# A hybrid streaming encoder step on one core: the windowed attention is cut by pairs of heads and interleaved with the query projection

## The chip, the cores and the metric

The kernel runs on one core of one Trainium2 chip. The metric is the device time of one execution in microseconds (us). An execution is one launch; TensorE (PE), VectorE (DVE), ScalarE (ACT), GpSimd (POOL) and the DMA queue of SyncE (SP) each follow their own instruction list and meet only at semaphores.

## The reference, cut to what matters

One step of a two-layer encoder over 256 prompt frames and 64 new frames (T = 320 tokens, 1024 channels). Layer 0 is a recurrent mixer and a mixture of experts (MoE); layer 1 is attention over a window of three chunks of 64 frames, with 16 query heads on 4 key/value heads and a learned sink per head, and again a MoE.

```python
def sink_probs(s, sink, mask):
    m = jnp.maximum(jnp.max(s, axis=-1, keepdims=True), sink)
    e = jnp.exp(s - m)
    return e / (jnp.sum(e, axis=-1, keepdims=True) + jnp.exp(sink - m))

def window_attn(h, pos, k, v, past_k, past_v, p, j):
    q = (h @ p['at_w_q'][j] + p['at_b_q'][j]).reshape(B, S, N_HEADS, HEAD_DIM)
    q = rope_partial(q, pos)
    ...            # scores of each 64-frame chunk with its own and the two chunks before it
    probs = sink_probs(s, sink, mask)
    o = jnp.einsum('bnkgqs,bnskd->bnqkgd', probs, vb)
    return o.reshape(B, T, H * hd) @ p['at_w_o'][j] + p['at_b_o'][j]
```

The 320 tokens are five chunks (n = 0 to 4): the prompt's four, which see 64, 128, 192 and 192 keys, and the new frames' one, which sees 192 (128 cached, 64 own).

## The kernel before, in words

Everything is stored with channels on the 128 partitions: the residual is `x[:, c, :]` with C = 8 blocks of 128 channels and 320 tokens. A block of queries holds two heads of 64, a pair. Each engine's work is one hand-written list in one function; a helper notes under which key an instruction counts its engine's semaphore up, and `wait(key)` waits for that count. So the order of the code is the order on each engine, and an engine that waits holds up all that stands behind it. `bank.open` hands out the eight PSUM banks in turn.

In the profile every matmul of TensorE has the line L677 (the helper `mm`), transposes have their own (L1180 for the probabilities), every ACT operation L1224, and DVE's L1477 (tensor with tensor), L1480 (tensor with scalar) and L1483. A 32-bit matmul shows as two records. The form "128*128 128x320" is a 128 by 128 weight tile and an operand of 320 columns; "64*64" and "128*64" are smaller tiles of the array.

Layer 1's mixer goes like this:

- The keys are rotated, turned and copied (until about 869 us).
- `project("q", [c], ...)` makes the queries of pair c: 8 matmuls, 16 records. ACT adds the bias (`qraw`), `q_turn(c)` multiplies by the constant matrix `ropep` on TensorE, and DVE finishes the rotation with three operations (`q ready`). TensorE runs the eight projections first, each turn one pair behind.
- Then the five chunks. `scores(n)` makes the scores of chunk n for all 16 heads. DVE `row_maxima(n)` takes maxima and adds the sink, ACT `exps(n)` takes 8 exponentials and one of the sink, DVE divides, TensorE turns the probabilities 64 keys at a time (`attended(n)`, first half), ACT copies the turned blocks `pT` out of PSUM, TensorE multiplies by the values `v64` (second half), ACT copies the result to `oT`. TensorE's list holds `scores(n + 1)` ahead of `attended(n)`.
- `project("ao", ...)`, the output projection, waits for all of `oT`; then the MoE of layer 1.

The DMA queue of SP loads the second half of the output projection's weights and the first experts' weights when the query weights have been used.

## Time and profile before

| what | value |
|---|---|
| time before, median of 3 runs | 1338.46 us (1337.78 to 1346.84) |
| profiled execution | 1344.89 us, of which the span of its instructions 1343.1 us |
| TensorE busy in the span | 1150.3 us (86%), mean granted clock 0.93 |
| DVE, ACT busy | 540.1 us (40%), 343.9 us (26%) |
| query projection to output projection | 869.5 to 973.6 us |

The span runs from the first to the last instruction of the profiled execution; the rest of its time lies around it. Busy shares are means over stages with different limits, so a change in one stage has to be read in that stage. The granted clock is TensorE's: 1.00 is 2.4 GHz, 0.50 is 1.2 GHz, and a number between is a stretch that holds both.

### The profile page before, as it was taken

To read this page: it belongs to the slowest core of one execution; us is meant where nothing else is said; L and a number is where in the kernel's file an instruction comes from. 1 tells how busy PE (TensorE), PEld (TensorE's weight loads), DVE (VectorE), ACT (ScalarE), POOL (GpSimd) and SP (SyncE) were. 2 spreads that over 40 slices of the span, in tenths; PEclk is the share of its full clock that TensorE was granted. 3 is DMA by queue.
4 is the path that set the end of the run, shared out by engine and by line. 5 is a ranking of instruction groups with operands and counts; after the bars stand their busy time and mean duration, and the time that the engine had idled before them with its cause. 6 is when DMAs were issued, how large, how long until landed. Compare 5 with 4: busy or idle time off the path is not lost.

```text
span 1343.1 us, 23574 instructions
## 1 busy us (share of the span) xinstructions
PE 1150.3 (86%) x9621; PEld 675.5 (50%) x9621; DVE 540.1 (40%) x1412; ACT 343.9 (26%) x652; POOL 57.0 (4%) x67
## 2 busy tenths in 40 slices
PE   5579998888988878689999997897795899999995
PEld 2146665565767744434444443575672534444433
DVE  3422193333331254524444544325227235444444
ACT  1122230121111201223333223215303232323322
POOL 2000000000000000001000001000000000000100
PEclk9789998999898988889999999898697999999997
DMA  9533115867674144039999997006022079999941
GB/s 250 164 125 126 63 62 197 292 232 263 227 256 182 39 189 180 1 125 418 429 423 426 425 380 259 6 6 251 1 94 94 0 320 423 427 426 422 424 184 39
DMA packets 45992, 297.19 MB, mean 221 GB/s; under 512 B 5972, under 2 KB 7352, under 8 KB 22360
## 3 DMA queue, kind: packets, MB, share of 16 engines
q1 hardware_dynamic: 43856, 290.17, 54.4%
q0 software_dynamic: 1856, 5.79, 1.9%
q8 instruction: 63, 1.03, 0.3%
q10 hardware_dynamic: 200, 0.06, 0.0%
q14 instruction: 17, 0.14, 0.0%
HBM read 293.77 MB, written 2.24 MB: 220 GB/s over the span
## 4 chain that ended last, share of the span: by engine, by line
PE 75%; DMA 10%; DVE 9%; ACT 3%; issue 2%; SPq 0%; ACTq 0%; DVEq 0%; POOL 0%; POOLq 0%
PE bank L677 73%; DMA ring<-in_ada_w 8%; DVE work L1477 3%; ACT work L1224 2%; DMA ring<-in_kv_ada_w 1%; DVE work L1483 1%; DVE work L1480 1%; DVE rstd L1515 1%; DVE x_res L1850 1%; DMA ring<-in_rw_w_rkv 1%; PE bank L1055 1%; DVE work L1836 1%; DVE ring L1477 1%; DVE att L1927 1%; DVE work L1589 0%
## 5 line engine op out<-in xcount | busy, mean ns | idle before, releaser
L677 PE MATMUL bank<-ring,work 128*64 128x512 f32 (+1 forms) x1760 | 354.5, 558 | 9.3 <-DVE work L1836 7.6
L677 PE MATMUL bank<-work,ring 128*128 128x320 f32 (+3 forms) x1600 | 300.3, 366 | 31.6 <-DVE work L1477 8.9
L677 PE MATMUL bank<-work 128*128 128x320 bf16 (+7 forms) x1842 | 238.7, 304 | 49.0 <-DVE work L1757 13.9
L677 PEld LDWEIGHTS bank<-work,ring 128*128 128x128 f32 (+2 forms) x1600 | 214.0, 173 | 118.5 <-issue 29.3
L677 PEld LDWEIGHTS bank<-work 128*128 128x128 bf16 (+2 forms) x1842 | 178.3, 132 | 118.0 <-issue 34.3
L677 PEld LDWEIGHTS bank<-ring,work 128*64 128x64 f32 (+1 forms) x1760 | 120.7, 141 | 220.7 <-issue 213.7
L1224 ACT ACTIVATE work<-bank 128x320 f32<-128x320 f32 (+6 forms) x116 | 59.1, 550 | 259.8 <-PE bank L677 234.2
L677 PE MATMUL bank<-ring 64*64 64x64 f32 (+2 forms) x2624 | 104.7, 234 | 2.0 <-issue 2.0
L677 PEld LDWEIGHTS bank<-ring 64*64 64x64 f32 (+2 forms) x2624 | 94.9, 145 | 22.8 <-issue 19.0
L677 PE MATMUL bank<-ring,cs 128*32 128x512 f32 x448 | 66.8, 675 | 34.9 <-DMA ring<-in_ada_w 29.0
L1850 DVE SCALAR_TENSOR_TENSOR x_res<-bank,mod,x_res 128x256 f32<-128x256 f32 (+1 forms) x256 | 86.2, 378 | 18.4 <-PE bank L677 4.6
L1830 DVE SCALAR_TENSOR_TENSOR work<-work,small,bank 128x256 f32<-128x256 f32 x32 | 21.5, 672 | 174.2 <-ACT work L1388 88.9
L1224 ACT ACTIVATE ring<-bank 128x512 f32<-128x512 f32 (+3 forms) x67 | 37.7, 563 | 191.0 <-PE bank L677 189.9
L1843 DVE TENSOR_TENSOR work<-bank,work 128x512 f32<-128x512 f32 x64 | 44.1, 689 | 61.9 <-ACT work L1392 61.9
L1477 DVE TENSOR_TENSOR ring<-ring,bank 128x512 f32<-128x512 f32 x45 | 29.1, 685 | 84.0 <-PE bank L677 84.0
L631 POOL TENSOR_TENSOR work<-work 128x512 bf16<-128x512 f32 x32 | 36.4, 1159 | 547.4 <-ACT work L1396 547.4
L1392 ACT ACTIVATE work<-bank 128x512 bf16<-128x512 f32 x64 | 38.1, 596 | 49.3 <-PE bank L677 49.3
L1483 DVE SCALAR_TENSOR_TENSOR work<-work,vec 128x320 f32<-128x320 f32 x56 | 27.0, 547 | 52.9 <-PE bank L677 52.6
L1376 ACT COPY work<-work 128x512 f32 x64 | 39.3, 623 | 14.1 <-issue 14.1
L677 PEld LDWEIGHTS bank<-ring,cs 128*32 128x32 f32 x448 | 10.9, 112 | 62.6 <-DMA ring<-in_ada_w 42.4
L1396 ACT ACTIVATE work<-work 128x512 bf16<-128x512 f32 x64 | 40.1, 626 | 8.6 <-DVE work L1843 8.6
L1224 ACT ACTIVATE work<-x_res 128x640 f32<-128x640 f32 x20 | 14.7, 736 | 98.0 <-DVE x_res L1483 45.5
(183 smaller groups left out, 757.6 us busy)
## 6 DMA issues: line engine op xcount, KB each, us to landing
ring<-in_moe_w_gu SPq DMA_DIRECT2D x64, 2048.0 KB, 13.3
ring<-in_moe_w_down SPq DMA_DIRECT2D x64, 1024.0 KB, 13.8
ring<-in_ada_w SPq DMA_DIRECT2D x40, 1024.0 KB, 5.3
ring<-in_rw_w_rkv SPq DMA_DIRECT2D x6, 2048.0 KB, 7.7
ring<-in_ada_w SPq DMA_DIRECT2D x4, 2048.0 KB, 28.5
ring<-in_kv_ada_w SPq DMA_DIRECT2D x8, 1024.0 KB, 5.1
ring<-in_rw_w_o SPq DMA_DIRECT2D x2, 2048.0 KB, 11.4
ring<-in_at_w_q SPq DMA_DIRECT2D x2, 2048.0 KB, 13.8
```

What stands on the lines that cost most here:

```text
L631: eng.tensor_tensor(dpart[:, 0, 2, cols], rest[:, n, :], dpart[:, 0, 1, cols], ALU.subtract).then_inc(S["lo_ready0"], 1)
L677: return eng.matmul(out, l, r, start=start, stop=stop, **kw)
L1055: ins = eng.transpose(ps[0][:, 2 * P * u + P * f:2 * P * u + P * f + P], hid[:, u, P * f:P * f + P], ident)
L1224: ac.did(eng.activation(out, in_, f, **kw), *keys)
L1376: eng.copy(xe[:, u, :, 64 * v:64 * v + 64], xall[:, :, bass.ds(at, SLOTS)]).then_inc(S["xe_ready"], 1)
L1392: eng.activation(dpart[:, u, 0, 512 * n:512 * n + 512], ps[4 + n][:, :], ACT.Copy).then_inc(S["hi_ready"], 1)
L1396: eng.activation(dpart[:, u, 1, 512 * n:512 * n + 512], rest[:, n, :], ACT.Copy).then_inc(S["mid_ready"], 1)
L1477: op(eng.tensor_tensor(out, a, b, o_), *keys)
L1483: op(eng.scalar_tensor_tensor(out, a, s_, b, o1, o2), *keys)
L1830: eng.scalar_tensor_tensor(hid_w[:, u], silu[:, u, :].rearrange("p (q f) -> p q f", f=2), wslot[:, u:u + 1], ps[3 + 4 * u][:, FE:2 * FE].r ...
L1843: eng.tensor_tensor(rest[:, n, :], ps[4 + n][:, :], dpart[:, u, 0, 512 * n:512 * n + 512], ALU.subtract).then_inc(S["rest_ready"], 1)
L1850: ins = eng.scalar_tensor_tensor(x[:, c, t0:t0 + n], ps[(6, 1, 2)[c % 3]][:, t0:t0 + n], mod[:, l, r, 40 + c:40 + c + 1], x[:, c, t0:t0 + ...
```

## The change

The attention loop now runs over the eight pairs of heads instead of over the five chunks, and is mixed into the loop of the projections. Step s of the new loop does, on TensorE: the projection of pair s, the turning of the probabilities of pair s - 3 (`prob_turn`), the rotation matmul of pair s - 1, the scores of pair s - 2 for all five chunks, and the product with the values of pair s - 3 (`attended`). ACT and DVE have matching loops. Three steps behind the last projection (s = 8, 9, 10) finish the last three pairs.

With it, data is laid out anew: the values are kept as tiles of 128 tokens (`vtok`) where a chunk's window holds a pair of key chunks, so that a window of 192 keys is one part of 128 (`PAIR`) and one of 64 (`LONE`); a pair's probabilities for all chunks are one row of 768, in two buffers; eight transposes turn them, four of 128 and four of 64 columns, and ACT copies them out in two operations. The negated sink is computed once (`nsink`), so that three small DVE operations per chunk become one per pair, and ACT adds the sink as a bias. `oT` moves to another buffer, and the output projection waits for it block by block. Two of the stores to DRAM become one, so the counts of `out_written` drop by 16.

```diff
+SPAN = [(0, 64, 0, 0), (0, 128, 0, 64), (0, 192, 1, 0), (64, 256, 1, 192), (256, 448, 0, 192)]
+PCOL = [0, 64, 384, 576, 192]
+VTILES = [(0, 128), (64, 128), (128, 128), (192, 64), None, (256, 64)]
+PAIR = [None, (0, 0), (0, 1), (1, 2), (4, 3)]
+LONE = [(0, 0), None, (2, 1), (3, 2), (5, 3)]
...
-        hkv, haq, q, qt, oT = E[1], E[5], E[6], E[7], E[5]
+        hkv, haq, q, qt, oT = E[1], E[5], E[6], E[7], E[1]
...
-        v64 = work[0:64, 4 * B:4 * B + 7 * 256].rearrange("p (n d) -> p n d", n=7)
+        vtok = work[:, 4 * B:4 * B + 6 * 256].rearrange("p (n d) -> p n d", n=6)
...
-        prob2 = [work[:, a:a + 1536].rearrange("p (c s) -> p c s", c=C) for a in (0, 7 * B)]
-        pT = work[0:64, 1536:1536 + 3072].rearrange("p (w c s) -> p w c s", w=3, c=C)
+        prob2 = [work[:, a:a + 768] for a in (0, 768)]
+        qrot2 = [work[:, a:a + T] for a in (1536, 1536 + T)]
+        pT2 = [work[:, 7 * B + a:7 * B + a + 1024].rearrange("p (w n s) -> p w n s", w=2, n=4) for a in (0, 1024)]
...
-            for c in range(C):
-                project("q", [c], haq, lambda hf: ("wq", hf), ("h", "A1"))
-                if c:
-                    q_turn(c - 1)
-            q_turn(C - 1)
-            pe.wait("kswapped", 1)
-
-            def scores(n):
...
+            def scores(c):
+
+                g = c // 2
+                pe.wait("q ready", c)
+                for b in range(2):
+                    pb = bank.open("score", c, b)
+                    for n, (lo, hi, at, col) in enumerate(SPAN):
...
                         for h in range(2):
...
-                            ins = mm(pb[r, 256 * cc:256 * cc + hi - lo], q[r, c, t0:t0 + CH],
+                            ins = mm(pb[r, col:col + hi - lo], q[r, c, CH * n:CH * n + CH],
                                      kT[r, var + g // 2, lo:hi], True, True)
...
-            def attended(n):
...
-            scores(0)
-            for n in range(NCH):
-                if n + 1 < NCH:
-                    scores(n + 1)
-                attended(n)
-            pe.wait("oT", NCH - 1)
-            project("ao", range(C), oT, lambda hf: ("ao", hf))
...
+            def prob_turn(c):
+
+                pe.wait("prob", c)
+                prob = prob2[c % 2]
+                pb = bank.open("pT", c, 0)
+                for n in range(1, NCH):
+                    ins = eng.transpose(pb[:, P * (n - 1):P * n], prob[:, PCOL[n]:PCOL[n] + P], ident)
+                full(ins, "pT", c, 0)
+                pb = bank.open("pT", c, 1)
+                for k, n in enumerate((0, 2, 3, 4)):
+                    a = PCOL[n] + (P if n else 0)
+                    ins = eng.transpose(pb[0:64, P * k:P * k + P], prob[:, a:a + 64], ident)
+                full(ins, "pT", c, 1)
+
+            def attended(c):
+
+                g = c // 2
+                pe.wait("pT ready", c)
+                pT = pT2[c % 2]
+                pb = bank.open("o", c)
+                for k, table, w in ((P, PAIR, 0), (64, LONE, 1)):
+                    for n in range(NCH):
+                        if table[n] is None:
+                            continue
+                        tile, at = table[n]
+                        for h in range(2):
+                            ins = mm(pb[64 * h:64 * h + 64, CH * n:CH * n + CH],
+                                     vtok[0:k, tile, 64 * g:64 * g + 64], pT[0:k, w, at, 64 * h:64 * h + 64],
+                                     w == 0 and n == 1, w == 1 and n == NCH - 1)
+                full(ins, "o", c)
+
+            pe.wait("kswapped", 1)
+            pe.wait("vtok")
+            for s in range(C + 3):
+                if s < C:
+                    project("q", [s], haq, lambda hf: ("wq", hf), ("h", "A1"))
+                if s >= 3:
+                    prob_turn(s - 3)
+                if 1 <= s <= C:
+                    q_turn(s - 1)
+                if 2 <= s <= C:
+                    scores(s - 2)
+                if s >= 3:
+                    attended(s - 3)
+                if s == C:
+                    scores(C - 1)
+            project("ao", range(C), oT, lambda hf: ("ao", hf), ("oT",))
...
-            for c in range(C):
...
-            def exps(n):
...
-            exps(0)
-            for n in range(NCH):
-                parts = min(n + 1, 3) if n < 4 else 3
-                for w in range(3):
-                    if w == 2 and n + 1 < NCH:
-                        exps(n + 1)
...
+            def exps(c):
+
+                prob, att = prob2[c % 2], att2[:, c % 2]
+                ac.wait("row max", c)
+                for n, (lo, hi, b, col) in enumerate(SPAN):
+                    act(prob[:, PCOL[n]:PCOL[n] + hi - lo], ps[seen_bank(("score", c, b))][:, col:col + hi - lo],
+                        ACT.Exp, ("read", "score", c, b), ("exp", c), bias=att[:, 1, n:n + 1], scale=SCALE,
+                        accum_out=att[:, 2, n:n + 1])
+                act(att[:, 3, 0:NCH], att[:, 1, 0:NCH], ACT.Exp, ("sink exp", c), bias=sink[:, c:c + 1])
+
+            for s in range(C + 3):
+                if s < C:
+                    act(q[:, s, :], pk("q", s)[:, 0:T], ACT.Identity, ("read", "q", s), ("qraw", s),
+                        bias=vcol("at_b_q", s))
+                if s >= 3:
+                    c = s - 3
+                    pT = pT2[c % 2]
+                    act(pT[:, 0], pk("pT", c, 0)[:, :].rearrange("p (n s) -> p n s", n=4), ACT.Copy,
+                        ("read", "pT", c, 0))
+                    act(pT[0:64, 1], pk("pT", c, 1)[0:64, :].rearrange("p (n s) -> p n s", n=4), ACT.Copy,
+                        ("read", "pT", c, 1), ("pT ready", c))
+                if s == C:
+                    exps(C - 2)
+                if s >= 3:
+                    act(oT[:, s - 3, :], pk("o", s - 3)[:, 0:T], ACT.Copy, ("read", "o", s - 3), ("oT", s - 3))
+                if 2 <= s < C:
+                    exps(s - 2)
+                if s == C:
+                    exps(C - 1)
...
-            for c in range(C):
-                tt_(qt[:, c, :], acst("sin"), pk("qrot", c)[:, 0:T], M, ("read", "qrot", c))
+            eng.wait_ge(in_sems["sink_in"], 32)
...
+            def rotated(c):
+
+                tt_(qrot2[c % 2], acst("sin"), pk("qrot", c)[:, 0:T], M, ("read", "qrot", c))
                 tt_(q[:, c, :], q[:, c, :], acst("cos"), M)
                 ve.settle()
-                tt_(q[:, c, :], q[:, c, :], qt[:, c, :], A_, ("q ready", c))
-            eng.wait_ge(in_sems["sink_in"], 32)
-
-            def row_maxima(n):
...
-                stt(att[:, 1, :], att[:, 0, :], SCALE, sink[:, :], M, ALU.max)
...
-                ts(att[:, 1, :], att[:, 1, :], -1.0, None, M, ALU.bypass)
...
-                tt_(att[:, 4, :], sink[:, :], att[:, 1, :], A_, *[("row max", n, b) for b in range(4)])
-
-            row_maxima(0)
-            for n in range(NCH):
-                W = min(n + 1, 3) * CH if n < 4 else 192
...
+            def row_maxima(c):
+
+                att = att2[:, c % 2]
+                a, b = [pk("score", c, k) for k in range(2)]
+                for n, w, col in ((0, 64, 0), (1, 128, 64), (4, 192, 192)):
+                    op(eng.tensor_reduce(att[:, 0, n:n + 1], a[:, col:col + w], AX.X, ALU.max))
+                op(eng.tensor_reduce(att[:, 0, 2:4], b[:, 0:384].rearrange("p (n s) -> p n s", n=2), AX.X, ALU.max))
+                ve.settle()
+                ts(att[:, 1, 0:NCH], att[:, 0, 0:NCH], -SCALE, nsink[:, c:c + 1], M, ALU.min, ("row max", c))
...
+            def normalized(c):
+
+                prob, att = prob2[c % 2], att2[:, c % 2]
+                ve.wait("sink exp", c)
+                tt_(att[:, 5, 0:NCH], att[:, 2, 0:NCH], att[:, 3, 0:NCH], A_)
...
+                op(eng.reciprocal(att[:, 5, 0:NCH], att[:, 5, 0:NCH]))
...
+                for n, (lo, hi, _b, _col) in enumerate(SPAN):
+                    a = slice(PCOL[n], PCOL[n] + hi - lo)
+                    ts(prob[:, a], prob[:, a], att[:, 5, n:n + 1], None, M, ALU.bypass, ("prob", c))
+
+            for s in range(1, C):
+                rotated(s - 1)
+                if s >= 2:
+                    row_maxima(s - 2)
+                    normalized(s - 2)
+            rotated(C - 1)
+            for c in (C - 2, C - 1):
+                row_maxima(c)
+            for c in (C - 2, C - 1):
+                normalized(c)
```

TensorE's order before, from the last two projections (`work,ring` 128x320) over the rotation matmuls (`work,const_phase`) to the scores and products of the first chunks (64x64 to 64x192) and the turnings (L1180):

```order
L677 MATMUL bank<-work,ring 128x320 x8
L677 MATMUL bank<-work,const_phase 128x320
L677 MATMUL bank<-work,ring 128x320 x8
L677 MATMUL bank<-work,const_phase 128x320 x2
L677 MATMUL bank<-work 64x64 x16
L677 MATMUL bank<-work 64x128 x16
L1180 MATMUL bank<-const,work 64x128 x8
L677 MATMUL bank<-work 64x128 x8
L677 MATMUL bank<-work 64x192 x16
```

All projections stand ahead of all attention, and the turnings of a chunk ahead of its product. In the changed kernel, step s = 7, the last of the five full ones, from its projection to the next step's first turnings (L1183 and L1188 are the two sizes of turnings):

```order
L686 MATMUL bank<-work,ring 128x320 x8
L1183 MATMUL bank<-const,work 128x128 x4
L1188 MATMUL bank<-const,work 64x128 x4
L686 MATMUL bank<-work,const_phase 128x320
L686 MATMUL bank<-work 64x64 x2
L686 MATMUL bank<-work 64x128 x2
L686 MATMUL bank<-work 64x192 x6
L686 MATMUL bank<-work 64x64 x16
L1183 MATMUL bank<-const,work 128x128 x4
```

Turnings, rotation, scores and products of three different pairs now stand between two projections. What remains behind the last one, from the products of pair 5 with the scores of pair 7 to the output projection (`work,ring` x64):

```order
L686 MATMUL bank<-work 64x64 x18
L686 MATMUL bank<-work 64x128 x2
L686 MATMUL bank<-work 64x192 x6
L1183 MATMUL bank<-const,work 128x128 x4
L1188 MATMUL bank<-const,work 64x128 x4
L686 MATMUL bank<-work 64x64 x16
L1183 MATMUL bank<-const,work 128x128 x4
L1188 MATMUL bank<-const,work 64x128 x4
L686 MATMUL bank<-work 64x64 x16
L686 MATMUL bank<-work,ring 128x320 x64
```

The last two pairs' turnings and products stand there with nothing between them. On ACT before, one chunk's exponentials (`work,att`) and its sink, then copies of turned probabilities (64x512) and of the result (128x8x64):

```order
L1224 ACTIVATE work,att<-bank,att 128x192 x8
L1224 ACTIVATE att<-att 128x8
L1224 ACTIVATE work<-bank 64x512 x2
L1224 ACTIVATE work<-bank 128x8x64
L1224 ACTIVATE work<-bank 64x512 x4
```

Here the exponentials of a chunk stand ahead of most copies of the chunk before. On ACT in the changed kernel, step s = 7: bias of the queries, two copies of turned probabilities, copy of the result (128x320), five exponentials and the sink:

```order
L1245 ACTIVATE work<-bank,vec 128x320
L1245 ACTIVATE work<-bank 128x512
L1245 ACTIVATE work<-bank 64x512
L1245 ACTIVATE work<-bank 128x320
L1245 ACTIVATE work,att<-bank,att 128x64
L1245 ACTIVATE work,att<-bank,att 128x128
L1245 ACTIVATE work,att<-bank,att 128x192 x3
L1245 ACTIVATE att<-att,sink 128x5
```

The copy of one pair's result now stands ahead of the next pair's exponentials.

## Rows read from the trace of the kernel before

**Rows 1.** The page: span, TensorE's busy time and share.

```profile
span 1343.1 us, 23574 instructions
PE 1150.3 (86%) x9621; PEld 675.5 (50%) x9621; DVE 540.1 (40%) x1412; ACT 343.9 (26%) x652; POOL 57.0 (4%) x67
```

**Rows 2.** Windows by stage: length, busy time (instructions) of each engine, PEclk, DMA share, GB/s.

```profile
869.50:908.00 38.50, 38.42 (x144) 26.83 (x143) 8.47 (x19) 4.99 (x12) 3.17 (x6) 1.00 0.05 11
908.00:962.00 54.00, 38.42 (x357) 32.13 (x359) 23.77 (x91) 27.79 (x107) 0.00 (x0) 0.77 0.39 157
962.00:974.00 12.00, 10.54 (x98) 9.11 (x96) 0.00 (x0) 4.52 (x8) 0.00 (x0) 0.76 0.01 1
```

**Rows 3.** Chain that ended last, in order of time: start us, us, what.

```profile
869.55 38.24 PE bank L677 x142
...
937.68 3.33 ACT work L1224 x16
...
942.10 9.67 PE bank L677 x76
951.76 0.03 issue
...
951.89 1.96 DVE att L1927 x4
...
973.56 39.04 PE bank L677 x144
```

**Rows 4.** Windows of single TensorE runs between chunks, columns as in Rows 2.

```profile
924.80:926.90 2.10, 1.99 (x17) 1.67 (x16) 1.83 (x4) 1.39 (x3) 0.00 (x0) 1.00 0.87 367
...
942.10:951.80 9.70, 9.70 (x81) 8.63 (x82) 1.40 (x7) 0.60 (x1) 0.00 (x0) 0.56 0.01 2
951.60:953.70 2.10, 2.00 (x17) 1.67 (x16) 1.81 (x4) 1.37 (x3) 0.00 (x0) 1.00 0.00 0
...
958.90:964.80 5.90, 5.90 (x49) 5.57 (x50) 1.40 (x7) 0.00 (x0) 0.00 (x0) 0.50 0.00 0
...
969.70:972.90 3.20, 3.11 (x48) 2.86 (x48) 0.00 (x0) 0.01 (x1) 0.00 (x0) 1.00 0.03 5
```

**Rows 5.** Timeline, one projection, its rotation and the next: start, us, engine line op.

```profile
878.54 4.47 PE L677 MATMUL bank<-work,ring 128*128 128x320 f32 x16
...
882.85 0.70 PE L677 MATMUL bank<-work,const_phase 128*128 128x320 f32 x2
...
883.39 4.47 PE L677 MATMUL bank<-work,ring 128*128 128x320 f32 x16
883.59 0.49 DVE L1477 TENSOR_TENSOR work<-const_phase,bank 128x320 f32<-128x320 f32 x1 [3.43 <-PE bank L677]
...
884.51 0.49 DVE L1477 TENSOR_TENSOR work<-work 128x320 f32<-128x320 f32 x1
```

**Rows 6.** Timeline, small matmuls at full clock and the weight loads after a change of tile.

```profile
908.59 0.92 PE L677 MATMUL bank<-work 64*64 64x64 f32 x24
...
924.85 1.67 PEld L1180 LDWEIGHTS bank<-const,work 128*64 128x64 f32 x16 [0.28 <-issue]
924.85 1.94 PE L1180 MATMUL bank<-const,work 128*64 128x128 f32 x16
```

**Rows 7.** Groups by form, 869.5 to 973.6 us: busy us, mean ns, idle before.

```profile
L677 PE MATMUL bank<-work 64*64 64x192 f32 x96 | 13.9, 446 | 0.0
...
L1927 DVE TENSOR_REDUCE att<-bank 128x2 f32<-128x384 f32 x12 | 5.9, 550 | 10.8 <-PE bank L677 10.8
L1480 DVE TENSOR_SCALAR work<-work,att 128x192 f32<-128x192 f32 x24 | 5.8, 315 | 0.1
...
L1942 DVE RECIPROCAL att<-att 128x8 f32<-128x8 f32 x5 | 1.0, 203 | 0.2
...
L1224 ACT ACTIVATE work<-bank 64x512 f32<-64x512 f32 x24 | 12.8, 590 | 14.1 <-PE bank L1180 14.0
...
L1224 ACT ACTIVATE work<-bank,vec 128x320 f32<-128x320 f32 x8 | 4.2, 527 | 33.5 <-PE bank L677 33.5
...
L1224 ACT ACTIVATE att<-att 128x8 f32<-128x8 f32 x5 | 1.2, 242 | 0.0
```

**Rows 8.** DMA queue of SP and landing times of the output projection's weights.

```profile
907.27 0.37 SPq L485 DMA_DIRECT2D ring<-in_at_w_o  x1
...
ring<-in_at_w_o SPq DMA_DIRECT2D x2, 2048.0 KB, 14.1
```

More of the change, by code:

```diff
@@ L263, in build @@
         sink = sb("sink", [P, C])
+        nsink = sb("nsink", [P, C])
         att2 = sb("att", [P, 2, 6, C])
@@ L655, in _ @@
                 put(o[n_out][0, t0:t0 + 64].rearrange("t n d -> t (n d)"), k64[:, w, :])
-            pl.wait("v64")
-            for n_out, w, t0 in ((5, 2, 0), (5, 3, 64), (9, 6, 0)):
-                put(o[n_out][0, t0:t0 + 64].rearrange("t n d -> t (n d)"), v64[:, w, :])
+            pl.wait("vtok")
+            put(o[5][0].rearrange("t n d -> t (n d)"), vtok[:, 2, :])
+            put(o[9][0].rearrange("t n d -> t (n d)"), vtok[0:64, 5, :])
             cleared(1)
@@ L1132, in _ @@
             pe.wait("vT", 1)
-            for w, t0 in enumerate((0, 64, 128, 192, 256)):
-                pb = bank.open("v64", w)
+            for w, tile in enumerate(VTILES):
+                if tile is None:
+                    continue
+                t0, k = tile
+                pb = bank.open("vtok", w)
                 for c in range(2):
-                    ins = eng.transpose(pb[0:64, P * c:P * c + P], vT[:, c, t0:t0 + 64], ident)
-                full(ins, "v64", w)
+                    ins = eng.transpose(pb[0:k, P * c:P * c + P], vT[:, c, t0:t0 + k], ident)
+                full(ins, "vtok", w)
             for w, t0 in enumerate((128, 192, 384)):
@@ L1424, in _ @@
                 act(kT[:, 2 + c, :], pk("kswap", c)[:, 0:448], ACT.Copy, ("read", "kswap", c), ("kswapped", c))
-            for w in range(5):
-                act(v64[:, w if w < 4 else 6, :], pk("v64", w)[0:64, 0:256], ACT.Copy, ("read", "v64", w), ("v64",))
+            for w, tile in enumerate(VTILES):
+                if tile is not None:
+                    act(vtok[0:tile[1], w, :], pk("vtok", w)[0:tile[1], 0:256], ACT.Copy, ("read", "vtok", w),
+                        ("vtok",))
             for w in range(3):
@@ L1428, in _ @@
                 act(k64[:, w, :], pk("k64", w)[0:64, 0:256], ACT.Copy, ("read", "k64", w), ("k64",))
-            for c in range(C):
-                act(q[:, c, :], pk("q", c)[:, 0:T], ACT.Identity, ("read", "q", c), ("qraw", c),
-                    bias=vcol("at_b_q", c))
-            def exps(n):
-                W = min(n + 1, 3) * CH if n < 4 else 192
-                prob, att = prob2[n % 2], att2[:, n % 2]
-                for b in range(4):
-                    ac.wait("row max", n, b)
-                    for cc in range(2):
-                        c = 2 * b + cc
-                        act(prob[:, c, 0:W], ps[seen_bank(("score", n, b))][:, 256 * cc:256 * cc + W], ACT.Exp,
-                            ("read", "score", n, b), ("exp", n, c), bias=att[:, 1, c:c + 1], scale=SCALE,
-                            accum_out=att[:, 2, c:c + 1])
-                act(att[:, 3, :], att[:, 4, :], ACT.Exp, ("sink exp", n))
```

64 lines of the change are left out of this document (9 added, 55 removed).

## The prediction

> **What bounds the kernel now.** I read the page first [rows 1]: TensorE is busy for 86% of the span, but that is a mean over many stages. The windows by stage come next [rows 2]. In the query projection TensorE is busy for 38.42 of 38.50 us at full clock; nothing can be gained there without taking work away. In the 66 us behind it TensorE is busy for 49 us, at a granted clock of 0.77 and 0.76, while DVE (23.8 us) and ACT (27.8 + 4.5 us) are idle for more than half. The chain of waits [rows 3] says why: it runs from TensorE to DVE's maxima to ACT's exponentials and back, chunk by chunk, and no engine has another chunk's work to fill with. From the first projection (869.55) to the output projection (973.56) it is 104.0 us. The third thing is the clock [rows 4]: from 942.1 to 951.8 TensorE is busy throughout but mostly at half clock, and from 958.9 to 964.8 wholly at half clock, both right behind a pause. A clock of 0.77 over 54 us and 0.76 over 12 us means that about 46% of the 66 us ran at 1.2 GHz.
>
> **The change: work of a full step at full clock.** From one projection to the next is 4.85 us for 18 equal records [rows 5], so 16 records of projection are 4.3 us and a rotation 0.54 us. Turnings: 16 took 1.94 us [rows 6], so 8 are 0.95 us; there are 64 in place of 96. The scores keep their columns: 768 keys for 2 heads in 2 records each. At full clock 48 records of 128 columns took 3.11 us [rows 4], 0.032 us for 64 columns (0.038 by the 24 records in 0.92 us of [rows 6], which contain the last one's own length). 48 such units are 1.55 us. The products with the values fall from 256 records of 128 columns to 256 of 64 over the whole stage; 32 a step make 1.05 us, if the two heads of a pair run side by side as they do in those rows.
>
> New is that the size of the array's tile changes within a step: into the scores, into the products of 128 keys, into those of 64, and back to the projection. The nearest row is the weight loader's pause of 0.28 us between 64*64 and 128*64 tiles [rows 6]. Part of such a pause is the usual spacing, so I take 0.1 us each, between 0 and 0.28. The step is 4.3 + 0.95 + 0.54 + 1.55 + 1.05 + 0.4 = 8.8 us.
>
> The Trainium skill, page "TensorEngine Tiling", section "Tiling Modes" (Key Properties), says that a change of tiling mode, unlike one of the tile alone, makes TensorE drain. The pause of 0.28 us is in line with a short drain. If each drain showed the whole length of a small record, 0.446 us [rows 7], the four would cost 1.8 us a step in place of 0.4, and the gain below would be about 8 us smaller.
>
> **The chain of a full step.** TensorE may finish its own work early and still wait for the next probabilities, so I follow one pair from the start of its neighbour's rotation matmul (0). DVE begins 0.74 us later (882.85 to 883.59) and needs 1.41 us for three operations (883.59 to 884.51 + 0.49) [rows 5]: 2.15. The scores end on TensorE at 0.54 + 0.1 + 1.55 = 2.2. The reductions, one of 0.55 us [rows 7] and three smaller, overlap a little: I put 1.15, and 0.2 for the sink: 3.5. The products end at 3.45, and ACT's list has the copy of their result, 0.53 us [rows 7], ahead of the exponentials: ACT is free at 4.1. Eight exponentials of 192 keys take 3.33 us [rows 3], 0.42 each; three of these and two smaller are 1.9, and the sink's 0.24 [rows 7] brings 6.25. DVE adds, takes the reciprocal (0.2) and divides five times, 0.24 each (24 in 5.8 us) [rows 7]: 7.8. The turnings follow, 0.95: 8.75. Chain and TensorE's own work are level, so the step is 8.8 us, and each of the two hides the other. If only the chain grew, by a longer product for instance, it would show in full. The copies of turned probabilities, 2 x 0.59 us [rows 7], lie beside rotation and scores (2.1 us).
>
> **The whole stage.** Fill: three projections and a rotation put the second pair's rotation at 13.45; the first chain lacks the copy ahead of the exponentials and ends at 20.65, TensorE's fourth projection at 19.95; with the turnings the third rotation stands at 21.6. Four steps of 8.8 lead to 56.8, where the last full step's rotation stands; pair 5's probabilities are ready at 64.6. TensorE has had nothing since 60.25, a pause of 4.35 us.
>
> Behind the projections: turnings 0.95, rotation 0.54, scores of pair 6 1.65, products of pair 5 1.15, scores of pair 7 1.55, that is 70.4; maxima 1.45 with the delay, exponentials 2.15: 74.0. ACT copies pair 6's turned probabilities only then (1.2), products 1.15, turnings of pair 7 0.95, their copies 0.9 past the end, products 1.15: 79.4. The output projection can start, since it needs pair 7 only for its eighth matmul. At full clock the gain is 104.0 - 79.4 = 24.6 us.
>
> Then the clock. That tail holds 9.1 us of TensorE work in 15 us, behind a pause of 4.35 us. Before, with pauses like that, 46% of the stage ran at half clock [rows 2]; I take two thirds for the tail, +6.1 us, and 1.5 us for the start of the output projection, of which a first block of 4.3 us would be 8.6. The ends are 0 and 9.1 + 4.3. Gain: 24.6 - 7.6 = 17 us.
>
> **What moves and costs nothing.** The second half of the output weights is loaded when the last query weights have been used, at 907.27 before [rows 8], some 55.6 us into the stage now, about 925. They land 14.1 us later, and the fifth block of the output projection comes 17 us behind its start at 957: covered by 35 us. The experts' first loads stand behind it on SP's queue and move by the same 18 us, with over 100 us to their use. GpSimd's two stores in place of three leave at a time when nothing waits for them. TensorE's new wait for the copied values ahead of the projections has the projections behind it; the copies ran beside the turnings before, so I put 0, at most the 0.4 us of one copy. Waiting for `oT` block by block costs nothing. A PSUM bank comes round after eight openings, and a step has seven, so each was read a step earlier.
>
> **The sum.** The profiled execution took 1344.89 us with a span of 1343.1, 6.4 us above the median of 1338.46; the gain belongs to one stage, and I take it off both. Profile: span 1343.1 - 17 = 1326; median 1321.5.
>
> **Rivals.**
> *The clock holds in the tail.* Before, it was still at 1.00 in a short run of turnings right behind scores (951.6 to 953.7) [rows 4]. Then the gain is 24.6 us: 1314. Against it stands the long pause.
> *The step is longer.* If the two heads' products don't overlap where 128 rows of the array are used (+1.05 us), or tile changes cost 0.28 and more (+0.7), a step is 9.5 to 10.5 us, since products and tile changes lie on the chain as well; over six steps the gain falls by 4 to 10 us: 1326 to 1332. That is what the page on tiling would make of it.
> *Half clock in the full steps* (the slower side). The projections no longer stand together; between them are 4.5 us of small tiles, and small tiles ran at 0.50 and 0.56 in [rows 4]. At half clock a step's TensorE work would be 17 us, 8.4 more. Two of the five steps eat the gain; all five give 1321.5 + 42 = 1363. Against it: those rows began behind a pause, half of each step is full-size projection, which ran at 1.00 [rows 2], and turnings behind scores held 1.00 twice [rows 4].
> *It doesn't interleave*: some wait puts one pair's chain behind the other's, so that a step takes 8.8 plus the chain's other half, 4 us; five steps more or less return the gain: 1338.
>
> **How the numbers follow.** Forecast 0.48, the clock holds 0.22, longer steps 0.18, half clock in the steps 0.06, no interleaving 0.06. The likeliest is 1321.5. The bounds are a gain of 27 us (no tile costs, full clock) and of about 1 us (every bound at its bad end at once); 8 in 10 reach from 1313 to 1333. About 1%, 13.4 us, is what a measurement of this kernel can tell from no change. Faster by over that: 0.22 + 0.44 of the forecast's 0.48 + 0.03 of the longer steps' = 0.69; within it 0.04 + 0.15 + 0.06 = 0.25; slower 0.06.
>
> **What would show it.** Right: the stage from the first query projection to the output projection is 85 to 90 us; full steps repeat every 8.8 us with TensorE's clock at 1.00; a pause of some 4 us stands behind the last projection, and the clock is at half in the tail. Maxima, exponentials and divisions of each pair lie under the next projection. Wrong: steps above 9.5 us, with TensorE waiting for DVE's divisions ahead of the turnings; half clock during projections; or a change outside the stage, which I have put at nothing.

## The result and the profile after

| kernel, in one comparison | median | runs | range |
|---|---|---|---|
| before | 1338.36 us | 4 | 1337.78 to 1346.84 |
| changed | 1324.91 us | 4 | 1324.00 to 1325.82 |

The ratio is 0.987, with an interval of 0.9846 to 0.9894: faster, by 13.5 us by these medians, where 17 were forecast. The profiled execution took 1324.0 us, and its page begins so:

```profile
span 1321.8 us, 23637 instructions
...
PE 1131.9 (86%) x9653; PEld 659.4 (50%) x9653; DVE 542.0 (41%) x1424; ACT 341.3 (26%) x650; POOL 56.4 (4%) x66
```

TensorE's share of the span is 86% as before [rows 1]; its busy time fell by 18.4 us and the span by 21.3. The page doesn't tell where, so the stage comes next. From the first record of the query projection to the first of the output projection it was 869.39 to 973.56, 104.2 us; now it is 868.83 to 952.38, 83.6 us. The windows by stage (length, busy us and instructions of PE, PEld, DVE, ACT and POOL, then TensorE's granted clock, DMA share, GB/s):

```profile
869.00:890.80 21.80, 20.93 (x96) 14.55 (x96) 5.64 (x18) 6.31 (x20) 2.73 (x5) 1.00 0.08 19
890.80:925.30 34.50, 34.50 (x315) 25.45 (x314) 17.03 (x60) 16.03 (x61) 0.00 (x0) 1.00 0.00 1
925.30:932.70 7.40, 3.31 (x55) 2.29 (x54) 4.23 (x15) 3.23 (x14) 0.00 (x0) 1.00 0.98 361
932.70:943.00 10.30, 7.24 (x82) 5.35 (x82) 5.54 (x21) 5.08 (x22) 0.00 (x0) 0.83 1.01 427
943.00:952.30 9.30, 7.87 (x80) 6.32 (x80) 1.51 (x8) 3.55 (x10) 0.00 (x0) 0.52 0.36 147
952.30:957.00 4.70, 4.70 (x13) 3.05 (x10) 0.00 (x0) 0.44 (x1) 0.00 (x0) 0.50 0.00 0
957.00:993.70 36.70, 36.66 (x137) 25.55 (x135) 10.78 (x28) 4.23 (x5) 0.00 (x0) 1.00 0.31 119
```

The first line is the fill, the second the full steps: 34.5 us in which TensorE never stops, at full clock, with 17 us of DVE and 16 of ACT beside it. Before, 54 us of attention held 38 us of TensorE work at 0.77 [rows 2]. Then come three lines of tail, with pauses in the first two and half clock in most of the last two, and one in which the output projection still starts at 0.50.

The timeline of TensorE (start, us, instructions, idle time before and who ended it) shows a step and the tail:

```profile
889.88 0.66 PE L1183 MATMUL bank<-const,work 128*128 128x128 f32 x4 [0.87 <-DVE work L1504]
...
898.54 0.60 PE L1183 MATMUL bank<-const,work 128*128 128x128 f32 x4
898.97 0.60 PE L1188 MATMUL bank<-const,work 128*64 128x128 f32 x4
899.41 0.70 PE L686 MATMUL bank<-work,const_phase 128*128 128x320 f32 x2
900.04 2.75 PE L686 MATMUL bank<-work 64*64 64x64 f32 x52
902.73 4.57 PE L686 MATMUL bank<-work,ring 128*128 128x320 f32 x16
907.14 0.60 PE L1183 MATMUL bank<-const,work 128*128 128x128 f32 x4
...
932.78 0.86 PE L1183 MATMUL bank<-const,work 128*128 128x128 f32 x4 [4.17 <-DVE work L1504]
...
943.07 0.91 PE L1183 MATMUL bank<-const,work 128*128 128x128 f32 x4 [3.06 <-DVE work L1504]
...
945.52 2.17 PE L686 MATMUL bank<-work 128*64 128x64 f32 x32 [0.68 <-ACT work L1245]
...
952.38 32.94 PE L686 MATMUL bank<-work,ring 128*128 128x320 f32 x113
```

From turnings to turnings a step is 8.60 us (898.54 to 907.14). No record in it has an idle time. Only the first turnings (0.87 us, the fill) and those behind the last projection (4.17 and 3.06 us) wait for DVE's divisions at L1504. The same group of 32 products takes 2.17 us here that takes 1.30 us at full clock (below). The output projection starts without waiting for anything. How close the other side of a step is shows on DVE:

```profile
905.79 1.14 DVE L1504 TENSOR_SCALAR work<-work,att 128x64 f32<-128x64 f32 x5
...
914.39 1.14 DVE L1504 TENSOR_SCALAR work<-work,att 128x64 f32<-128x64 f32 x5
```

The divisions end at 906.93 and the turnings begin at 907.14; the next pair's end at 915.53 and its turnings begin at 915.74. That is 0.21 us, of which some 0.05 also lie between the two where the turnings do wait (914.28 to 914.32 in the longer chain below). So the chain of a pair is done 0.1 to 0.2 us before TensorE comes to it.

### The profile page after: what moved, and what is told of

Same layout as the page of the kernel before. It is cut to its first block, busy times and chain, and to the rows that moved or that the text cites. A ratio compares the mean times of both kernels' runs of the same rounds, so it can differ in the third digit from the quotient of the medians.

```text
span 1321.8 us, 23637 instructions
## 1 busy us (share of the span) xinstructions
PE 1131.9 (86%) x9653; PEld 659.4 (50%) x9653; DVE 542.0 (41%) x1424; ACT 341.3 (26%) x650; POOL 56.4 (4%) x66
## 3 DMA queue, kind: packets, MB, share of 16 engines
q8 instruction: 64, 1.05, 0.3%
## 4 chain that ended last, share of the span: by engine, by line
PE 75%; DMA 11%; DVE 9%; ACT 2%; issue 2%; SPq 0%; ACTq 0%; DVEq 0%; POOL 0%; POOLq 0%
PE bank L686 73%; DMA ring<-in_ada_w 9%; DVE work L1501 2%; DMA ring<-in_kv_ada_w 2%; ACT work L1245 1%; DVE work L1507 1%; DVE work L1504 1%; DVE rstd L1539 1%; DVE x_res L1874 1%; DMA ring<-in_rw_w_rkv 1%; PE bank L1064 1%; DVE work L1860 1%; DVE ring L1501 1%; DVE work L1613 0%; PE bank L1231 0%
## 5 line engine op out<-in xcount | busy, mean ns | idle before, releaser
L686 PE MATMUL bank<-work 128*128 128x320 bf16 (+7 forms) x1906 | 227.0, 284 | 41.8 <-DVE work L1781 13.9
L686 PEld LDWEIGHTS bank<-work 128*128 128x128 bf16 (+3 forms) x1906 | 166.8, 126 | 113.2 <-issue 39.7
L1245 ACT ACTIVATE work<-bank 128x320 f32<-128x320 f32 (+6 forms) x111 | 55.8, 537 | 252.4 <-PE bank L686 235.8
## 6 DMA issues: line engine op xcount, KB each, us to landing
ring<-in_moe_w_gu SPq DMA_DIRECT2D x64, 2048.0 KB, 13.5
```

Of the source, the lines that this page charges most:

```text
L686: return eng.matmul(out, l, r, start=start, stop=stop, **kw)
L1245: ac.did(eng.activation(out, in_, f, **kw), *keys)
```

## The experiments

The table reads each run's trace at the same three points: the first record of the query projection, the first of the output projection, and the last. "At half" is the length times twice what the granted clock lacks to 1.00, that is, the time at 1.2 GHz. The ratio is to the kernel before, run beside it.

| kernel | first projection at | stage, us | at half, us | output projection, us | median us | ratio, interval |
|---|---|---|---|---|---|---|
| before | 869.39 | 104.2 | 30.7 | 34.7 | 1338.36 | 1 |
| changed | 868.83 | 83.6 | 12.5 | 37.0 | 1324.91 | 0.987 (0.9846 to 0.9894) |
| before, again | 867.81 | 104.2 | 30.7 | 34.7 | 1343.33 | one run |
| pairs apart | 870.20 | 91.0 | 16.5 | 36.7 | 1327.30 | 0.985 (0.9812 to 0.9886) |
| warm tail | 872.54 | 78.7 | 0 | 34.7 | 1320.19 | 0.981 (0.978 to 0.9834) |
| longer chain | 873.50 | 90.5 | 16.0 | 36.9 | 1333.36 | 0.990 (0.9863 to 0.9933) |
| changed, again | 863.64 | 83.6 | 12.5 | 37.0 | 1323.22 | 0.986 (0.982 to 0.9899) |
| early output | 863.86 | 78.7 | 0 | 28.3 | 1308.82 | 0.976 (0.9723 to 0.9805) |
| before, warm | 867.07 | 95.0 | 0 | 34.7 | 1333.62 | 0.993 (0.9904 to 0.9957) |
| more tile changes | 871.07 | 90.1 | 12.2 | 37.1 | 1327.50 | 0.989 (0.986 to 0.9922) |
| pairs apart, warm | 867.89 | 88.9 | 3.4 | 34.7 | 1325.97 | 0.988 (0.9845 to 0.9921) |

The stage repeats within 0.1 us in the two profiles of the kernel before and in the two of the changed kernel. Where it begins does not: 868.83 and 863.64 us in the two executions of the changed kernel, up to 873.50 in the others. The kernel before had medians of 1338.36, 1346.81, 1342.93 and 1340.51 us in the four comparisons. So sizes below are told by the stage, and by the median only where it can tell.

One difference lies outside stage and output projection. These are the windows from 39.0 us (before) and 41.3 us (changed) behind the start of the output projection, which is the same place in both programs, to the end:

```profile
1012.60:1343.10 330.50, 283.49 (x1468) 133.18 (x1468) 148.80 (x454) 101.13 (x173) 20.84 (x20) 0.94 0.66 277
...
993.68:1321.80 328.12, 281.25 (x1468) 132.52 (x1468) 148.93 (x454) 101.12 (x173) 20.82 (x20) 0.95 0.67 279
```

This part, mostly the MoE, is 2.4 us shorter with the same 1468 records of TensorE and a granted clock of 0.95 instead of 0.94. It repeats: from the end of the output projection to the end of the span it is 334.8 us in both profiles of the kernel before and 332.5 in both of the changed one, 2.3 us less. No run shows why the clock is higher there.

### The kernel before and the changed kernel, each once more

No edit.

> The unchanged kernel before, for a second profile. The profiled executions of before and after differ by 20.9 us (1344.89 and 1324.0), the medians by 13.5. Theory A: the execution of before that was profiled lost its 6.5 us over the median in the attention stage, by half clock; then this one, if its time is near 1338, shows the stage from the first query projection to the output projection at 97 to 99 us in place of 104.0, with less than 30 us at half clock. Theory B: the 6.5 us lie in other stages; then the stage is again 103 to 105 us while the span is near 1336.5, and the gain in the stage (20.6 us) is partly given back by half clock at the start of the output projection (about 2 us) and the rest is chance in the clock elsewhere.

The kernel before in windows of the stage and of the output projection, columns as above:

```profile
867.81:971.97 104.16, 87.08 (x594) 67.78 (x592) 32.22 (x109) 37.37 (x126) 3.16 (x6) 0.85 0.22 85
971.97:1006.70 34.73, 34.73 (x129) 24.59 (x130) 9.02 (x21) 2.21 (x3) 0.00 (x0) 1.00 0.23 91
```

The stage came back with the same length and the same clock. This execution took 1343.3 us, though, and not the 1338 that theory A asked for, so it can't rule A out by itself. It is 1.6 us shorter than the first, and its stage begins 1.6 us earlier. The clearer case is the changed kernel: its two profiled executions differ by 5.1 us (1324.0 and 1318.9), its stage begins 5.2 us earlier in the second, and is equally long. So what varied between the profiled executions of one kernel lies ahead of the stage, as theory B had it.

> The changed kernel unchanged, timed in more rounds beside the kernel before. In the first comparison the medians differ by 13.5 us; in the last job the kernel before ran between 1338 and 1349, median 1346.8, while its stage was 104.2 us in both profiles. Theory: the stage gains 20.6 us less 2.3 for the output projection's start at half clock in every execution, and the executions of either kernel vary by some 10 us ahead of the stage, so with more runs the difference of the medians is 16 to 22 us. Rival: the gain depends on the execution (half clock in the stage by chance), then stage lengths differ between profiles of the same kernel by more than 2 us and the difference stays at 13 to 14.

The changed kernel's stage was 83.6 us again, and the output projection 37.0. Its median, 1323.22 (1318.70 to 1326.55), is 19.7 us under that of the kernel before in the same comparison, 1342.93 (1336.07 to 1351.63), where the first comparison gave 13.5. From the first projection to the end of the output projection the gain is 138.9 - 120.5 = 18.4 us; with the 2.3 us behind it, 20.7 us from the first projection to the end of the span, above both medians' differences. The two comparisons' medians thus differ by 6 us, the two pairs of profiles, from the first projection on, by 0.1.

### Pairs, but not interleaved

All projections and rotations first, then pair after pair, the scores of one ahead of the turnings of the one before; ACT's and DVE's lists follow that order:

```diff
+            for c in range(C):
+                project("q", [c], haq, lambda hf: ("wq", hf), ("h", "A1"))
+                if c:
+                    q_turn(c - 1)
+            q_turn(C - 1)
+            scores(0)
+            for c in range(C):
+                if c + 1 < C:
+                    scores(c + 1)
+                prob_turn(c)
+                attended(c)
```

> All eight projections first, as in the kernel before, then the pairs, each pair's scores ahead of the turnings of the pair before; all else as in the changed kernel. Theory: the gain comes from the projections as cover. A pair's cycle without cover is divisions 1.55, maxima 1.45 and exponentials 2.15, 5.2 us, in which TensorE has 3.6 us of work at full clock and 7.2 at half; eight pairs of 5.5 to 7 us, 5 us ahead and 4 behind, on top of 38.4 us of projections: stage 92 to 103 us, time 1327 to 1338, TensorE at half clock for most of the pairs. Rival: cutting by pairs alone (fewer turnings, fewer columns in the products) makes the gain: then the time is at or below 1325.

TensorE's timeline of the first pairs and of two later ones:

```profile
916.60 0.66 PE L1183 MATMUL bank<-const,work 128*128 128x128 f32 x4 [4.28 <-DVE work L1496]
...
918.56 4.72 PE L686 MATMUL bank<-work 128*64 128x64 f32 x52 [0.68 <-ACT work L1243]
...
936.85 2.60 PE L686 MATMUL bank<-work 128*64 128x64 f32 x52 [0.73 <-ACT work L1243]
940.48 0.66 PE L1183 MATMUL bank<-const,work 128*128 128x128 f32 x4 [1.03 <-DVE work L1496]
...
945.92 0.66 PE L1183 MATMUL bank<-const,work 128*128 128x128 f32 x4 [1.02 <-DVE work L1496]
```

The stage is 91.0 us, just under the 92 to 103 that my theory allowed, and 16.5 us of it ran at half clock, not most of the pairs. A pair takes 5.44 us (940.48 to 945.92), of which TensorE waits 1.03 for the divisions and 0.73 for ACT's copies. The pairs with their new layout, not interleaved, bring 13.2 of the 20.6 us of the stage; mixing them into the projections brings the other 7.4. This run doesn't part the smaller unit from the layout that came with it.

### The clock held in the tail

Matmuls whose results nobody reads fill the two pauses, seven ahead of pair 5's turnings and five ahead of pair 6's:

```diff
+            def warm(k, n):
+                pb = bank.open("warm", k)
+                for _ in range(n):
+                    ins = mm(pb[:, 0:T], acst("ropep"), q[:, 0, :], True, True)
...
+                if s in (C, C + 1):
+                    warm(s - C, (7, 5)[s - C])
```

> The changed kernel with matmuls whose result nobody reads in the two pauses behind the last projection: 7 (14 records of 128x320) ahead of pair 5's turnings and 5 ahead of pair 6's. Theory: the pauses of 4.2 and 3.1 us bring TensorE to half clock for 17 us; filled, the clock stays at 1.00, the tail from 928.5 to the output projection shrinks from 23.9 to some 19 us, and the projection's start is no longer at half clock: 5 to 7 us less, 1318 to 1320. Rival: the small tiles and turnings of the tail bring it down whatever stands in the pauses, or the fillers delay the turnings: 1324 to 1327.

The filling and the turnings behind it on TensorE, then a product of the tail:

```profile
932.22 4.04 PE L686 MATMUL bank<-work,const_phase 128*128 128x320 f32 x14
936.46 0.65 PE L1183 MATMUL bank<-const,work 128*128 128x128 f32 x4 [0.21 <-DVE work L1514]
...
946.96 1.30 PE L686 MATMUL bank<-work 128*64 128x64 f32 x32 [0.72 <-ACT work L1255]
```

With 24 more records on TensorE the stage is 4.9 us shorter and the output projection 2.3 us: the product takes 1.30 us instead of 2.17. Pair 5's turnings begin 6.93 us behind the start of the scores ahead of them, as in the changed kernel (929.53 to 936.46, 925.85 to 932.78), and still wait 0.21 us: its divisions came no earlier and the filling held nothing up. What was won is the clock behind the pauses.

### A chain one microsecond longer

Three more exponentials of 192 keys, into a spare buffer, ahead of each pair's own:

```diff
+                for n in (2, 3, 4):
+                    lo, hi, b, col = SPAN[n]
+                    act(work[:, a3 + ...], ps[seen_bank(("score", c, b))][:, col:col + 192], ACT.Exp, ("spare", c, n),
+                        bias=att[:, 1, n:n + 1], scale=SCALE)
```

> The changed kernel with three more exponentials of 192 keys per pair on ACT, ahead of the needed ones, into a spare buffer: about 1.0 us more on the chain of each pair, nothing more on TensorE. Theory: chain and TensorE's own work are level within 0.2 us in a full step, so a step grows from 8.6 to 9.4 us and a pause of 0.8 us stands ahead of each turnings; with the first chain and two in the tail 6 to 8 us more: 1331 to 1333. Rival: the chain has slack to spare (TensorE alone bounds the step): only first chain and tail grow, 2 to 3 us, 1327 to 1328.

Two starts of TensorE's turnings with the rotation behind the first, and the divisions ahead of the second in the chain of waits:

```profile
904.90 0.66 PE L1183 MATMUL bank<-const,work 128*128 128x128 f32 x4 [0.60 <-DVE work L1509]
...
905.83 0.70 PE L686 MATMUL bank<-work,const_phase 128*128 128x320 f32 x2
...
914.32 0.66 PE L1183 MATMUL bank<-const,work 128*128 128x128 f32 x4 [0.60 <-DVE work L1509]
```

```profile
913.13 1.15 DVE work L1509 x5
914.28 0.04 issue
914.32 0.66 PE bank L1183 x4
```

The step is 9.42 us instead of 8.60, and now the divisions are waited for in each. From the rotation to the divisions it is 7.30 us (905.83 to 913.13) where it was 6.38 (899.41 to 905.79). So of 0.92 us put on the chain 0.1 went into its slack and 0.8 showed in the step. The stage grew by 6.9 us, within the 6 to 8 expected for chain and TensorE being level; the median of 1333.4 is just above the 1331 to 1333.

### Six more tile changes a step

The same products, in an order in which 128 keys and 64 keys alternate:

```diff
-                for k, table, w in ((P, PAIR, 0), (64, LONE, 1)):
-                    for n in range(NCH):
+                for n in (1, 0, 2, 3, 4):
+                    for k, table, w in ((P, PAIR, 0), (64, LONE, 1)):
```

> The changed kernel with the products of 128 and of 64 keys in turn, chunk by chunk, in place of all of 128 and then all of 64: 6 more changes of the array's tile per pair, 48 in all, and the same records. Theory: a change costs 0.1 us (records start 0.25 us apart where 0.16 is usual), so a pair's products grow by 0.5 to 0.7 us, a full step from 8.6 to 9.2, the stage from 83.6 to 88: 1329 to 1331. Rival, a full drain at each change: 0.28 us and more each, a step of 10.2 or more, 1337 to 1340. Third: changes are free, 1325.

Scores and products of a step on TensorE, and the turnings of two steps:

```profile
911.14 0.60 PE L1183 MATMUL bank<-const,work 128*128 128x128 f32 x4
...
912.64 3.63 PE L686 MATMUL bank<-work 64*64 64x64 f32 x52
...
920.62 0.60 PE L1183 MATMUL bank<-const,work 128*128 128x128 f32 x4
```

The 52 records take 3.63 us instead of 2.75, and the step 9.48 instead of 8.60. Six changes cost 0.88 us, 0.147 each, against 0.1 taken in the prediction and the 0.28 of its upper bound. Nothing was added but the order. The 0.88 us are more than the 0.5 to 0.7 expected, so step and stage (9.48 and 90.1 us) are longer than the 9.2 and 88 expected, while the median, 1327.5, lies under the 1329 to 1331 (a difference that the starts of the stage can make). By the Trainium skill, page "TensorEngine Tiling (Array Packing)", section "Tiling Modes" (Key Properties), a change of tiling mode drains TensorE; the trace agrees that a change costs, at about a third of a record's 0.446 us [rows 7].

### The clock held in the kernel before, and in pairs apart

Idle matmuls as above: in the kernel before six ahead of the first chunk's turnings and one to three ahead of each chunk's product; in pairs apart seven ahead of the first pair's turnings, then one ahead of each pair's turnings and one ahead of its products.

```diff
+            def warm(pb, k):
+                for _ in range(k):
+                    mm(pb[:, 0:T], acst("ropep"), q[:, 0, :], True, True)
...
+                        pb = bank.open("pT", n, w, hf)
+                        if n == 0 and hf == 0:
+                            warm(pb, 6)
...
+                pb = bank.open("o", n)
+                warm(pb, (1, 3, 3, 3, 1)[n])
                 pe.wait("pT ready", n)
-                pb = bank.open("o", n)
```

> The kernel before with idle matmuls in most of its pauses of TensorE, written into the PSUM bank that the waiting work will overwrite: 6 ahead of the first chunk's turnings, 1 to 3 ahead of each chunk's product. Theory: of its 104.2 us stage, 30.7 at half clock, TensorE's runs at half clock cost 10 to 13 us, and with the clock held the stage is 91 to 95 us, as short as the pairs without cover (91.0); so much of what cutting by pairs gains is the clock. Rival: the products of 64 keys on half of the array's rows keep the clock at half whatever stands ahead of them, or the chain of engines sets the length: 100 to 105 us.

> The pairs behind the projections (no interleaving), with idle matmuls in TensorE's pauses: 7 ahead of the first pair's turnings, then one ahead of each pair's turnings and one ahead of its products. With the clock held in all three, the stages would be 95.0 us (kernel before with idle matmuls), X here, 78.7 us (changed kernel with idle matmuls). Theory: cutting by pairs shortens the cycle by itself, from fewer turnings, narrower products, fewer small operations on DVE and equal pairs; without cover a pair's cycle is 5.45 us and X is 87 to 89: about 7 us from the pairs, 9 from the projections as cover. Rival: without the half clock the pairs bring nothing over the chunks, X is 93 to 96, and their 13 us in the stage were the clock alone.

Two products of the kernel before behind their filling, on TensorE:

```profile
925.41 1.88 PE L677 MATMUL bank<-work,const_phase 128*128 128x320 f32 x6 [1.92 <-ACT work L1231]
927.23 4.56 PE L677 MATMUL bank<-work 64*64 64x128 f32 x64
...
937.10 1.88 PE L677 MATMUL bank<-work,const_phase 128*128 128x320 f32 x6 [0.18 <-ACT work L1231]
938.94 5.43 PE L677 MATMUL bank<-work 64*64 64x128 f32 x80
```

And the chain of waits of two pairs in pairs apart, warm:

```profile
919.73 0.67 PE bank L1188 x4
...
920.43 2.90 ACT work L1249 x12
...
924.35 0.78 DVE work L1502 x3
...
925.18 0.67 PE bank L1188 x4
...
925.87 2.90 ACT work L1249 x12
```

The run of TensorE that took 9.7 us in the kernel before [rows 4] takes 5.4, and the stage 95.0 instead of 104.2. One filling cost time of its own: that of chunk 1 could start only when its PSUM bank was free (925.41, behind a pause of 1.92), when ACT's copies for the products had ended 1.2 us before, and put the products off by 1.82 us to 927.23. Without it the stage would be up to 1.8 us shorter, an estimate from these two rows. In pairs apart the stage went from 91.0 to 88.9, within the 87 to 89 expected: its pairs still repeat every 5.44 us (920.43 to 925.87), set by ACT's copy and exponentials, the divisions and the first turnings, one behind the other, which no filling shortens. With the clock held, or nearly (3.4 us at half are left in pairs apart), the three ways stand at 93.2 to 95.0 (chunks), 88.9 (pairs) and 78.7 us (pairs among projections).

### Work of the next stage in the pauses

The last run puts useful work where the idle matmuls were: twelve matmuls of the output projection, on the pairs that are done by then, in two PSUM banks that are kept until pairs 6 and 7 are added.

```diff
+                if s == C:
+                    early(0, range(0, 5))
+                    early(1, range(0, 2))
+                if s == C + 1:
+                    early(1, range(2, 5))
+                    early(0, [5])
+                    early(1, [5])
...
+            for m in range(2):
...
+                for c in (6, 7):
+                    pe.wait("oT", c)
+                    ins = mm(ps[seen_bank(("ao", m))][:, 0:T], ..., oT[:, c, :], False, c == 7)
...
+            project("ao", range(2, C), oT, lambda hf: ("ao", hf), ("oT",))
```

> The changed kernel with part of the output projection moved into the two pauses behind the last query projection: 7 matmuls of its first two blocks ahead of pair 5's turnings, 5 ahead of pair 6's; the two PSUM banks are held until the blocks are finished. Theory: the pauses are filled with useful work, the clock stays at 1.00 as with the idle matmuls (stage 78.7), and 12 matmuls of 0.54 us are gone from the output projection: from the first query projection to the end of the output projection 107 us in place of 113.4 with idle matmuls and 120.5 in the changed kernel; 1311 to 1315. Rival: the held banks or the waits for copied results hold up scores and turnings of the last pairs: 1317 to 1322.

The two fillings and the output projection behind them on TensorE:

```profile
923.58 4.04 PE L687 MATMUL bank<-work,ring 128*128 128x320 f32 x14
927.82 0.66 PE L1184 MATMUL bank<-const,work 128*128 128x128 f32 x4 [0.20 <-DVE work L1531]
...
933.37 3.04 PE L687 MATMUL bank<-work,ring 128*128 128x320 f32 x10
936.51 0.66 PE L1184 MATMUL bank<-const,work 128*128 128x128 f32 x4
...
942.60 28.33 PE L687 MATMUL bank<-work,ring 128*128 128x320 f32 x104
```

The stage is as short as with idle matmuls, 78.7 us, and the output projection lasts 28.3 instead of 34.7, since 24 records of it are done. From the first projection to its end it is 107.1 us, as expected, 13.4 less than in the changed kernel; the medians of the same comparison differ by 14.4 (1308.82 against 1323.22), which puts this one under the 1311 to 1315 expected. This version beats both kernels: by 34 us that before.

## Why the prediction was right

**Bound and mechanism.** Right. The attention waited, and at half clock; the projections now lie over the chains. In the full steps TensorE has no wait and runs at 1.00, so the rival of half clock in the steps is out, and so is the one without interleaving; at 8.60 us a step, the rival of longer steps is out too.

**The step.** 8.8 us forecast, 8.60 measured. By the starts of its records that is 0.87 for the turnings (0.95 taken), 0.63 for the rotation (0.54), 2.69 for scores and products (900.04 to 902.73), where 3.0 were taken with the four tile changes, and 4.41 for the projection (4.3). A change costs 0.147 us by the run above, not 0.1; so scores and products themselves were shorter than taken. The two heads of a pair do run side by side: apart, the products would have taken 1.05 us more by the prediction's own rows. That chain and TensorE are level (8.75 and 8.8) is shown by the longer chain: 0.1 to 0.2 us of slack.

**Fill and tail.** The first turnings wait 0.87 us (20.65 - 19.95 = 0.7 forecast), the pause behind the last projection is 4.17 us (4.35 forecast). At full clock the stage was put at 79.4 us; with the clock held it measured 78.7.

**The clock** was the term with the widest bounds, 0 to 13.4 us, of which 7.6 were taken. It measured 7.2: 4.9 in the tail (6.1 taken) and 2.3 in the output projection (1.5 taken). The choice of "two thirds at half" from a stage that had 46% was a guess between bounds, and came out near; that the rival of a held clock was worth 7 us is shown by the warm tail.

**What moves and costs nothing.** The weights' loads fill the DMA engines from about 925 to 943 (shares of 0.98 and 1.01), where the prediction put them, and nothing in the stage waits for one.

**The size.** In what the forecast summed, it is right: the gain from first projection to the end of the output projection is 18.4 us, 17 forecast: of the 1.4 more, 0.7 are the stage at full clock, 0.4 the clock, 0.2 the stage before (104.2, not 104.0), and 0.1 rounding. A change outside the stage was put at nothing and named as a sign of being wrong. There is one, the 2.3 us behind the output projection. It happens to add to the gain, and the forecast had no term for it. The median of the first comparison showed less, 1324.9 against 1321.5, and that of the second a gain of 19.7. The profiles give 20.7 us from the first projection on both times, so the medians' difference is put down to what comes ahead of the stage; that is argued, since one execution of each run has a profile.

**What failed** is one rival, not the forecast: that without interleaving the gain would be gone (1338). Pairs apart, the nearest run to it, took 1327.3. That rival gave the whole gain to the cover by projections. The runs with the clock held divide it otherwise: 4.3 to 6.1 us come from the pairs and their layout (93.2 to 95.0, down to 88.9), some 10 from the cover (88.9 to 78.7), and the other 4.3 to 6.1 of the 20.6 in the stage from less time at half clock (9.2 to 11.0 lost in the kernel before, 4.9 in the changed one). The 3.4 us at half clock that are left in pairs apart could move up to 1.7 us from the cover to the pairs.

## What to carry to other kernels

When a stage is a chain across engines, cut it into units and put full work of a neighbouring stage between them, then compare the chain of one unit with the work between two: here 0.1 to 0.2 us of slack, so either one's growth shows. What is left uncovered is behind the last piece of cover; look there for a clock that falls with the pause, and fill it with the part of the next stage that is already ready, which was worth 13 us here, beside the 18 of the change itself. Where executions vary by 10 us ahead of the place that is changed, compare the stage's own length, and look behind the stage too: 2.3 us of this gain came in a part that the change doesn't touch.

## What was unexpected of the hardware

- In the kernel before TensorE was granted 0.56 over a run of products in which it was busy without a gap (942.1 to 951.8) [rows 4], behind a pause of 2.02 us. Within the run the clock was at half for most of the time and came back at its end, with nothing but these products on TensorE:

```profile
948.00:950.00 2.00, 2.00 (x16) 1.56 (x14) 0.00 (x0) 0.59 (x1) 0.00 (x0) 0.50 0.03 8
950.00:952.00 2.00, 2.00 (x20) 1.48 (x17) 0.11 (x1) 0.00 (x0) 0.00 (x0) 0.82 0.00 0
```

  With that pause and others before it filled by matmuls of a 128 by 128 tile and 320 columns, the same products ran in 5.43 us at 1.00. Whether the tile of the filling matters, or only that there is no pause, no run shows.
- In the changed kernel the clock stayed at 1.00 in the pause's own window (925.3 to 932.7) and half clock showed in the work behind it: 0.83, 0.52, and 0.50 for the first 4.7 us of a dense projection.
- A change of tile between 128 by 64 and 64 by 64 costs 0.147 us on average at full clock.
